# Who makes the low parts of three weight units in an attention mixer: VectorE or GpSimd

## What is computed

```
h = rms_norm(x, mix_norm[l])
u = h @ w_in[l]                                  # 18 weight units
y_conv = conformer_conv(...)                     # 31 taps, layer norm, silu
y_pool = multiscale_pool(...)                    # window sums
q, k = rms_norm(q), rms_norm(k)
for each of 4 heads:
    p = softmax(q k^T - slope * dist)            # two score maps a head
    a = p[0] - lam * p[1]
    o = a @ v
y_attn = rms_norm(o, attn_subln[l]) * (1 - lambda_init)
x = x + concat(y_conv, y_pool, y_attn) @ w_out[l]   # 8 weight units
```

## Time and profile before

| | us |
|---|---|
| median of 3 runs | 2158.64 |
| lowest, highest | 2158.43, 2158.94 |
| the profiled execution's own time | 2155.65 |
| its span in the profile | 2153.8 |
| TensorE busy | 2112.6 (98% of the span) |
| VectorE busy | 1513.5 (70%) |
| ScalarE busy | 1144.6 (53%) |
| GpSimd busy | 366.6 (17%) |

### The profile page before, as it was taken

How to read it: one execution, slowest core, us unless ns; L and a number is a source line. 1 busy time by engine, 2 the same in 40 slices (tenths; PEclk the granted TensorE clock), 3 DMA queues, 4 the chain that set the end, 5 groups by cost and what they waited for, 6 DMA issues and landing times.

```text
span 2153.8 us, 39015 instructions
## 1 busy us (share of the span) xinstructions
PE 2112.6 (98%) x13570; PEld 1800.4 (84%) x13570; DVE 1513.5 (70%) x2382; ACT 1144.6 (53%) x1951; POOL 366.6 (17%) x462
## 2 busy tenths in 40 slices
PE   8999999999999999999999999999999998999998
PEld 7888888888888888888888988888888777868887
DVE  6666977667667966667667757667766787677666
ACT  5455755546446754555546446455654553355445
POOL 1111211112111211112111002111111102301111
PEclk9999999999999999999999999999999999999999
DMA  7655435555655345555556554656555452035653
GB/s 252 198 183 188 142 125 200 192 195 170 200 183 195 110 155 196 186 172 204 190 187 229 181 176 166 193 186 219 200 191 189 147 187 82 14 109 201 194 182 130
DMA packets 104401, 376.70 MB, mean 175 GB/s; under 512 B 11764, under 2 KB 12276, under 8 KB 104180
## 3 DMA queue, kind: packets, MB, share of 16 engines
q1 hardware_dynamic: 104308, 375.42, 51.6%
HBM read 373.29 MB, written 1.05 MB: 174 GB/s over the span
## 4 chain that ended last, share of the span: by engine, by line
PE 86%; DVE 7%; ACT 4%; issue 2%; POOL 1%; DMA 1%; SPq 0%; DVEq 0%; POOLq 0%; ACTq 0%
PE bank L939 27%; PE bank L943 14%; PE bank L188 13%; PE bank L189 13%; PE bank L190 12%; DVE w_lo L182 2%; ACT act L478 1%; DMA work<-pt_dram 1%; PE bank L1222 1%; ACT w_hi L175 1%; DVE act L588 1%; PE bank L2215 0%; DVE x L573 0%; PE bank L388 0%; PE bank L2205 0%
## 5 line engine op out<-in xcount | busy, mean ns | idle before, releaser
L939 PE MATMUL bank<-act,w_hi 128*128 128x512 f32 x2816 | 704.5, 392 | 3.8 <-DVE work L884 2.2
L939 PEld LDWEIGHTS bank<-act,w_hi 128*128 128x128 f32 x2816 | 515.0, 188 | 107.4 <-DVE act L588 4.2
L799 DVE TENSOR_TENSOR w_lo<-raw,w_hi 128x1024 fp32r<-128x1024 f32 x432 | 502.9, 1221 | 4.3 <-issue 1.0
L790 ACT ACTIVATE w_hi<-raw 128x1024 fp32r<-128x1024 f32 x432 | 425.0, 1050 | 2.4
L943 PEld LDWEIGHTS bank<-act,w_lo 128*128 128x128 f32 x2816 | 384.2, 190 | 27.6
L943 PE MATMUL bank<-act,w_lo 128*128 128x256 f32 x2816 | 392.6, 282 | 0.0
L890 DVE TENSOR_TENSOR work<-bank,work 128x256 f32<-128x256 f32 x176 | 74.8, 425 | 376.7 <-ACT work L820 376.7
L182 DVE TENSOR_TENSOR w_lo<-raw,w_hi 128x1024 fp32r<-128x1024 f32 x248 | 294.9, 1221 | 56.9 <-ACT w_hi L175 56.8
L851 POOL TENSOR_TENSOR work<-work,rb 128x256 f32<-128x256 f32 x176 | 129.5, 736 | 1037.9 <-DVE work L884 1037.9
L188 PE MATMUL bank<-w_hi,g_hi 128*128 128x512 f32 x704 | 277.2, 394 | 0.9 <-DVE w_lo L182 0.5
L189 PE MATMUL bank<-w_lo,g_hi 128*128 128x512 f32 x704 | 276.0, 392 | 0.0
(11 more groups left out here) (286 smaller groups left out, 2207.5 us busy)
## 6 DMA issues: line engine op xcount, KB each, us to landing
raw<-w_dram SPq DMA_DIRECT2D x680, 512.0 KB, 4.4
work<-rows_dram SPq DMA_DIRECT2D x13, 512.0 KB, 6.4
work<-rrows_dram SPq DMA_DIRECT2D x5, 512.0 KB, 4.4
x<-x_dram SPq DMA_DIRECT2D x2, 512.0 KB, 3.9
out<-x SPq DMA_DIRECT2D x4, 256.0 KB, 2.0
work<-work SPq DMA_DIRECT2D x2, 504.0 KB
work<-g_dram SPq DMA_DIRECT2D x1, 640.0 KB, 9.9
work<-dist_dram SPq DMA_DIRECT2D x2, 256.0 KB, 4.7
```

The source lines that it names most:

```text
L790: nc.scalar.activation(c.w_hi[:, n % RING, :], c.raw[:, n % RING, :], ACT.Copy).then_inc(c.hi_ready, 1)
L799: nc.vector.tensor_tensor(c.w_lo[:, n % RING, :], c.raw[:, n % RING, :], c.w_hi[:, n % RING, :].bitcast(F32), ALU.subtract).then_inc(c.lo_ ...
L939: nc.tensor.matmul(bank[:, :], c.w_hi[:, slot(m), k * P:(k + 1) * P], c.act[:, k, :, :], start=k == 0, stop=False)
```

## The change

A new helper `low_by_pool(pool, n)` makes the low part of unit n on GpSimd. It waits until `lo_ready` shows that unit n-1 is done and `hi_ready` that unit n has its high part, does the same subtraction on the same 128 x 1024 tiles, and counts `lo_ready`. VectorE's `split_lo` of W+2, W+3 and W+4 goes. GpSimd makes W+2 and W+3 behind its short windows, and W+4 behind the root of the first pair of heads. VectorE gets one wait: before its `split_lo` of W+5, for `lo_ready` of W+4.

```
+    def low_by_pool(pool, n):
+        pool.wait_ge(c.lo_ready, n)
+        pool.wait_ge(c.hi_ready, n + 1)
+        nc.gpsimd.tensor_tensor(c.w_lo[:, n % RING, :], c.raw[:, n % RING, :], c.w_hi[:, n % RING, :].bitcast(F32),
+                                ALU.subtract).then_inc(c.lo_ready, 1)
...
         c.split_lo(dve, W + 1)
         pool_low(dve)
-        c.split_lo(dve, W + 2)
         add_bias(dve, 2)
...
         add_bias(dve, 5)
-        c.split_lo(dve, W + 3)
         more_taps(dve, done, done + 2)
...
         more_taps(dve, done + 6, done + 10)
-        c.split_lo(dve, W + 4)
         more_taps(dve, done + 10, done + 15)
         mean_out(dve, 1)
         more_taps(dve, done + 15, len(taps))
+        dve.wait_ge(c.lo_ready, W + 5)
         c.split_lo(dve, W + 5)
...
         short_windows(pool)
+        low_by_pool(pool, W + 2)
+        low_by_pool(pool, W + 3)
         for pair in range(2):
             pool.wait_ge(*at("o_mean", pair + 1))
             nc.gpsimd.tensor_tensor(o_rstd[:, part], ...)
+            if pair == 0:
+                low_by_pool(pool, W + 4)
```

## The result

| | median us | lowest, highest | runs |
|---|---|---|---|
| before | 2157.79 | 2155.53, 2160.81 | 18 |
| changed | 2162.11 | 2159.02, 2167.05 | 18 |

The ratio is 1.0022, with a 95% interval of 1.0016 to 1.0028: the change costs 4.7 us, between 3.5 and 6.0 (4.3 by the difference of the medians). The forecast was 3.2 (2161.8), its range 2158.6 to 2165.2. The profiled execution of the changed kernel has a span of 2157.8 us, 4.0 over that of before.

What follows compares the result with a forecast made beforehand. TensorE was taken as the bound (86% of the chain). Saving 0, delays 0.6 + 1.0 = 1.6 us a mixer, 3.2 for two, on 2158.64 gave 2161.8 us; range 2158.6 to 2165.2.

Steps and rivals of the forecast that it cites:

- The saving is worth nothing: In the heads' middle, taking 7.3 us of low parts off VectorE gains 0, since TensorE's chain holds none of them.
- all three steps: Removing the low parts of W+2, W+3 and W+4 from VectorE, judged one by one: gain 0 each.
- The length of the GpSimd instruction: Each 128 x 1024 subtraction on GpSimd was taken to last 2.40 us, from a traced instruction of equal shape.
- the 2.96 of the rival: Rival: each GpSimd subtraction lasts up to 2.96 us, making 6.6 us in all, 2165.2; chance 0.16.
- The rule of exclusion: A VectorE instruction with both inputs in SBUF waits for a running GpSimd instruction's end; one reading PSUM does not.
- small steps pass: Rival: VectorE's 128 x 1 and 128 x 2 steps slip in beside GpSimd; 1.5 in all, 2160.1; chance 0.12.
- First place: Before head 0's turn: W+3 on GpSimd holds VectorE's lambda step 1.36 us; TensorE +0.6 us a mixer.
- Second place: Head 3's `mix_probs`: W+4 on GpSimd holds L1509 until 270.0, delaying W+2's product; TensorE +1.0 us a mixer.
- The clock: Rival: added waiting before W+2's product lowers TensorE's clock, 3.2 + 7 us, 2169; chance 0.04.
- The DMAs and the new wait before W+5: Shifted SyncE loads are used only near 300, and VectorE's wait before W+5 holds nothing: cost 0.
- within 0.2%: Outcome class: total time changes by no more than 0.2%, 4.3 us, either way; chance 0.80.

Runs made afterwards that it cites:

- e7: Changed kernel, but GpSimd's W+3 waits for the mixing of head 1 and W+4 for that of head 3: 2157.69 us, 1.0003.
- e5: Kernel before, plus three unread GpSimd subtractions a mixer on 128 x 1024 SBUF tiles where the change puts its three: 2162.00 us, 1.0021.
- e6: Kernel before, plus GpSimd work that only writes, three 128 x 768 memsets at each place where the change puts a subtraction: 2157.09 us, 1.0002.
- e2: Changed kernel with W+4 back on VectorE, so only W+2 and W+3 on GpSimd: 2158.90 us, 1.0007.
- e3: Changed kernel with W+2 and W+3 back on VectorE, so only W+4 on GpSimd: 2160.82 us, 1.0016.
- e1: Changed kernel measured once more, unaltered, against the kernel before: 2162.41 us, 1.0025.
- e8: Changed kernel with each GpSimd subtraction cut into four of 128 x 256, each waiting for the one before: 2161.82 us, 1.0020.

## Why the prediction was right, and where it was off

- *The saving is worth nothing.* Right at all three steps: idle time before the bias, before `mean_out`, and before `mix_probs` of head 2. e7 shows it in a time.
- *The length of the GpSimd instruction.* 2.40 was taken, 2.34 to 2.41 measured; the 2.96 of the rival was not met, and fp32r output costs nothing extra.
- *The rule of exclusion.* Right, and the rival "small steps pass" fell: an instruction on 128 x 1 waited 1.19 us. e5 and e6 add that GpSimd must read. The sentence of the Trainium skill ("SBUF — State Buffer", Who interferes with whom), that a two-input VectorE instruction contends with a GpSimd one that reads SBUF and not with one that only writes, agrees with both: 2.0 us a mixer for reads, 0.0 for writes. The root beside the taps is the exception that it doesn't name.
- *First place.* 0.6 predicted, 0.50 measured (e2). The lambda step was to be held 1.36 us and was held 1.19.
- *Second place.* 1.0 predicted, 0.65 measured (e3). The mis-sized term is how long L1509 is held, 1.25 predicted (268.75 to 270.0) and 0.99 measured (1.15 less its 0.16). It comes from the start and end of W+4: the prediction had it from 267.6 to 270.0 on its own scale, 267.43 to 269.78 by the trace put on that scale (0.25 added), because the root before it came 0.1 earlier with the smaller first place, and VectorE was let go before GpSimd's recorded end (269.53): L1509 ended at 269.55 with 0.16 of work still to do when it was let go, so at 269.39, or 269.64 on the scale of before, where 270.0 was taken. So 1.6 a mixer was 1.16, 3.2 in all was 2.3.
- *The clock.* This is the step that failed, and it made up for the others. The prediction gave a fall a chance of 4%, because in a wait of 3.8 us the clock had stayed at 1.00. That row came from one execution, and its window ends at 1790, 1.4 us before the wait does. Ten profiles here leave that wait empty (before, changed, and e1 to e8). In nine of them the clock goes to the lower level, beginning between 0.7 us before the wait's end and 1.4 us behind it, which such a row doesn't reach. The execution of before was the exception. The trace of before does hold a fall, in its last 3.8 us, where TensorE does nothing (granted clock 0.66). And the length of a single wait is a poor guide: in the mixer the longest is 0.97 us, and the clock still falls. Its price was over-sized as well: a third of 10 us a mixer; measured 1.25 to 1.6 a fall, in one mixer of the two in most executions profiled.
- *The total.* 3.2 forecast; 4.7 measured, of which 2.3 are the two delays and the rest is put down to falls of the clock. The size was near by luck: delays sized too large, falls left out. The time itself, 2161.8 for 2162.1, was nearer still by a second piece of luck: the forecast started from the 2158.64 of three runs, 0.85 above the median of 18. 80% was given to "within 0.2%"; the ratio, 1.0022, lies just past that, on the side that had 18%, and its interval covers the bound.
- *The DMAs and the new wait before W+5.* Cost 0, as said: VectorE was idle 1.54 before the convolution sum, as before (1.53). Matched matmul by matmul, TensorE is as late at 300 and 700 us as at 272 (1.15 to 1.16), so no load came too late.

What stays open: how often the clock falls in each mixer, since the timed runs give only their mean clock; why it falls in the second mixer and seldom in the first, with the same waits; how much of the loss belongs to the longer falls of the last layers; and what spares the taps beside the root.

## What to carry to other kernels

Before moving work to GpSimd, don't compare busy shares, but list what VectorE runs while GpSimd would read SBUF: each VectorE instruction with two SBUF inputs was held to the end of the GpSimd subtraction that it met, even one of 128 x 1 in a chain that TensorE waits for. The small root on GpSimd held nothing, so look at the durations and not at the engine alone. Put GpSimd's work beside VectorE's PSUM steps (e7), and don't cut it into pieces that meet the same chain again (e8). And if a delay lands where the matrix engine already does little, allow for a fall of its clock, and take the clock from several executions, not from one.

## What the runs showed of the hardware

- VectorE is released about 0.14 us before the recorded end of the GpSimd instruction: L1620 ended at 256.49 with its 0.15 of work, the GpSimd pair at 256.48.
- A reciprocal on 128 x 2, one SBUF input, is not held (0.17 us at 268.20, inside a GpSimd subtraction). Memsets on GpSimd hold nothing (e6: W+2's low part 1.22, lambda step 0.15), and neither does its root on 128 x 4 (three taps in 1.27 us beside it).
- At the seam of two GpSimd subtractions a waiting VectorE instruction gets in: in e5 W+2's low part waited for the first, ran (2.84 us in all), and the second waited for it (5.72 us for the pair, 4.86 where VectorE had nothing waiting).
- In the mixers the granted clock fell to 0.50 for 3.4 us each time and came back to 1.00; one fall at the product of W+2 cost 1.25 to 1.6 us. At the wait of 3.8 us it fell for 3.4 us too and cost about 0.8, because a later wait took up the rest. In the last layers it stayed low for 6.8 us in e2 and 10.2 in e1.
- Such falls differ from one execution to the next: nine of ten profiles have the one at the wait of 3.8 us.
